# Fourier output product from sums and differences of paired weight rows, in native float32 with the weights stationary

## The reference, cut to what matters

```python
def fourier_mix(h):                      # h: 256 tokens x 2048
    hg = h.reshape(B, L, FNET_GROUPS, FNET_GROUP_DIM)        # 8 groups of 256
    return jnp.fft.fftn(hg, axes=(1, 3)).real.reshape(B, L, D)
...
y_lat = fourier_mix(h_lat) @ fnet_w_out[slot]                # 2048 x 2048 weights
x = x + g1 * rms_norm(y_lat, norm_g[i, 1])
...
h = modulate(rms_norm(x, norm_g[i, 2]), sh2, sc2)            # then the MLP
```

## Time and profile before

| | |
|---|---|
| Time, median of 3 runs | 1682.26 us (1682.08 to 1682.56) |
| Profiled execution, first to last instruction (span) | 1678.7 us |
| PE busy | 1667.0 us, 99% of the span |
| DVE, ACT busy | 1190.8 us, 858.7 us |
| Mean granted clock of TensorE | 0.998 |

### The profile page before, as it was taken

The page is one execution under the profiler, slowest core; times in us unless marked ns, Lnnn a source line. Parts: engine busy times, 40 slices in busy tenths (PEclk is TensorE's granted clock), DMA queues, the critical chain, the costliest instruction groups (busy, mean ns, idle before and its releaser), DMA issues.

```text
span 1678.7 us, 22570 instructions
## 1 busy us (share of the span) xinstructions
PE 1667.0 (99%) x9084; PEld 1444.9 (86%) x9084; DVE 1190.8 (71%) x1291; ACT 858.7 (51%) x1212; POOL 21.3 (1%) x34
## 2 busy tenths in 40 slices
PE   9999999999999999999999999999999999999997
PEld 9899888888989988888898888888888888888886
DVE  7878777887868777798678577777655455546555
ACT  7667556444656655644464564434443444334442
POOL 0000000000100000000000000000000000000000
PEclk9999999999999999999999999999999999999999
DMA  9689676997777777799639478887655665566553
GB/s 333 215 274 313 218 272 226 335 356 279 247 258 253 267 238 263 240 346 370 228 125 334 151 226 282 294 286 245 196 176 200 187 190 197 210 196 188 189 200 126
DMA packets 218120, 408.16 MB, mean 243 GB/s; under 512 B 9088, under 2 KB 87200, under 8 KB 217248
## 3 DMA queue, kind: packets, MB, share of 16 engines
q1 hardware_dynamic: 217520, 404.58, 70.3%
q10 hardware_dynamic: 496, 2.14, 0.3%
HBM read 404.58 MB, written 2.11 MB: 242 GB/s over the span
## 4 chain that ended last, share of the span: by engine, by line
PE 97%; issue 1%; DVE 1%; ACT 0%; DMA 0%; POOL 0%; DVEq 0%; POOLq 0%; SPq 0%; ACTq 0%
PE banks L455 96%; PE banks L1663 1%; PE banks L1625 0%; DMA modw<-in_w_mod 0%; PE banks L1634 0%; DVE X L1104 0%; DVE X L1532 0%; PE banks L1821 0%; POOL sc L674 0%; ACT junk L712 0%; DVE modacc L1139 0%; ACT junk L723 0%; ACT swap L809 0%; ACT vtmp L1017 0%; ACT vtmp L1007 0%
## 5 line engine op out<-in xcount | busy, mean ns | idle before, releaser
L451 DVE TENSOR_TENSOR wlo<-raw,whi 128x1024 fp32r<-128x1024 f32 (+2 forms) x561 | 663.4, 1189 | 375.0 <-ACT whi L444 372.1
L444 ACT ACTIVATE whi<-raw 128x1024 fp32r<-128x1024 f32 (+2 forms) x561 | 573.4, 1030 | 578.4 <-PE banks L455 542.6
L455 PE MATMUL banks<-H,whi 128*128 128x512 f32 x2048 | 660.0, 398 | 0.7 <-DVE H L1062 0.7
L455 PEld LDWEIGHTS banks<-H,wlo 128*128 128x128 f32 x2048 | 384.9, 188 | 88.5
L455 PE MATMUL banks<-whi,Y 128*128 128x512 f32 x1472 | 455.6, 389 | 0.0
L455 PE MATMUL banks<-H,wlo 128*128 128x256 f32 x2048 | 402.6, 278 | 0.0
L455 PEld LDWEIGHTS banks<-whi,Y 128*128 128x128 f32 x1472 | 276.3, 188 | 57.7 <-DVE wlo L451 0.2
L455 PEld LDWEIGHTS banks<-H,whi 128*128 128x128 f32 x2048 | 317.0, 189 | 1.9 <-issue 0.8
L455 PE MATMUL banks<-wlo,Y 128*128 128x512 f32 x768 | 298.8, 389 | 0.0
L1139 DVE SCALAR_TENSOR_TENSOR modacc<-modw,cvx,modacc 128x1024 f32<-128x1024 f32 x188 | 240.4, 1279 | 9.7 <-DMA modw<-in_w_mod 9.4
L455 PEld LDWEIGHTS banks<-wlo,Y 128*128 128x128 f32 x768 | 144.2, 188 | 29.8
(11 more groups left out here) (224 smaller groups left out, 1343.5 us busy)
## 6 DMA issues: line engine op xcount, KB each, us to landing
modw<-in_w_mod SPq DMA_DIRECT2D x192, 512.0 KB, 6.5
raw<-in_w_in SPq DMA_DIRECT2D x72, 1024.0 KB, 5.4
raw<-in_w_mlp_in SPq DMA_DIRECT2D x64, 1024.0 KB, 5.5
raw<-in_w_mlp_out SPq DMA_DIRECT2D x64, 1024.0 KB, 5.0
raw<-in_w_o SPq DMA_DIRECT2D x32, 1024.0 KB, 7.1
raw<-in_w_fnet SPq DMA_DIRECT2D x16, 1024.0 KB, 5.1
raw<-in_w_mv SPq DMA_DIRECT2D x7, 1024.0 KB, 6.3
raw<-in_w_mk SPq DMA_DIRECT2D x6, 1024.0 KB, 6.1
```

Of the source, the lines that this page charges most:

```text
L444: nc.scalar.activation(hi_part(step, n), raw[u % RAW][:, (step % 2) * n:(step % 2) * n + n], ACT.Copy).then_inc(hi_ready, 1)
L451: nc.vector.tensor_tensor(wlo[u % RAW][:, part], raw[u % RAW][:, part], hi_part(step, n).bitcast(F32), ALU.subtract).then_inc(lo_ready, 1)
L455: return nc.tensor.matmul(o, a, b, start=start, stop=stop, skip_group_check=True)
```

## The change

The transform over features now gives, for each of 8 groups, only the outputs 1 to 128 (`PQ`, 32 native matmuls), and 16 more matmuls give output 0 of all groups (`P0`, 8 rows). Since output j and output 256 - j of a group are the same in their cosine part and opposite in their sine part, the product with `w_fnet` takes row j plus row 256 - j against the even part, and row j minus row 256 - j against the odd one. DVE makes these sums and differences (`fold`), and `dscale` halves row 128, which pairs with itself. The matmuls are native float32, with the folded weights stationary, and their result has features on the partitions; so ACT copies it out (`columns_out`), DVE makes all 256 frequencies (`unfold`), and PE transposes it to tokens (`tokens_of`). Rows 255 to 128 of each group are needed against rows 1 to 128, so 32 DMAs of 8 x 4 rows of 8 KB (`turn_rows`) write them in reversed order to `backward` in device memory, one with each of the load units 16 to 47 of layer 1. The product's last quarter is no longer done by token half, and the tail is written in another order. Twelve modulation units stand ahead of the product (`DFT_MODS`) and five in it, instead of 19 in it, and the pass's `mod_sums` stand behind it.

```diff
-BY_TOKEN = (FN_H - 8, ML_H - 8, END_H - 8)
+BY_TOKEN = (FN_H - 8, END_H - 8)
...
+DFT_MODS = [FN_H - 1 + (i + 1) / 16 for i in range(12)]
+TURN_AT = tuple(range(16, 48))
+BEFORE_MLP = ML_H - 0.5
...
-    for s in range(1, 22):
-        if s % 8:
-            yield FN_H + s
+    yield from DFT_MODS
+    for s in (2, 5, 13, 15, 21):
+        yield FN_H + s
...
-IDLE = 24
+IDLE = (12, 2)
...
+        PQ = at("PQ", [P, HEADS, SEQ], 0)
+        P0 = at("P0", [HEADS, SEQ], 16)
+        w0 = at("w0", [HEADS, D], 17)
+        own0 = at("own0", [P, 2 * HEADS], 30)
+        dscale = at("dscale", [P, 2], 30.25)
+        folded = [at(f"folded{i}", [P, 2, UNITW // 4], 96 + 4 * i) for i in range(HIR)]
...
+            if FN_H <= 2 * (u - RAW) < ML_H:
+                sp.wait_ge(fold_ready, 2 * (u - RAW) - FN_H + 2)
...
+            def turn_rows(i):
+                n = P // len(TURN_AT)
+                sp.dma_start(backward[:, i * n:(i + 1) * n, :], w_fnet.rearrange("(h r) n -> h r n", h=HEADS)[
+                    :, SEQ - 1 - i * n:SEQ - 1 - (i + 1) * n:-1, :]).then_inc(vec_in, 16)
...
+                        if l == DEPTH - 1 and at_unit in TURN_AT:
+                            turn_rows(TURN_AT.index(at_unit))
...
+            def load_pairs(v):
+                u, n, i = FN_H // 2 + v, v // 4, v % 4
+                if v < RAW:
+                    sp.wait_ge(half_used, 2 * (u - RAW) + 2)
+                else:
+                    sp.wait_ge(fold_ready, 2 * (v - RAW) + 2)
+                pairs = raw[u % RAW].rearrange("p (h e n) -> p h e n", h=2, e=2)
+                two, cols = slice(2 * i, 2 * i + 2), slice(512 * n, 512 * n + 512)
+                sp.dma_start(pairs[:, :, 0, :], rows_of_head[1:P + 1, two, cols]).then_inc(raw_in[u % RAW], 16)
+                sp.dma_start(pairs[:, :, 1, :], backward.rearrange("h p n -> p h n")[:, two, cols]).then_inc(raw_in[u % RAW], 16)
+            for at_step in DFT_MODS[:3]:
+                load_mod(at_step)
+            sp.wait_ge(vec_in, 32 + 16 * len(TURN_AT))
+            for v in range(16):
+                load_pairs(v)
+                if v == 0:
+                    sp.dma_start(w0[:, :], w_fnet.rearrange("(h r) n -> h r n", h=HEADS)[:, 0, :]).then_inc(vec_in, 16)
+                if v == RAW - 1:
+                    for at_step in DFT_MODS[3:]:
+                        load_mod(at_step)
+                load_mods(FN_H + 2 * v - MOD_LEAD)
...
-            for s in range(AHEAD):
-                split_hi(act, FN_H + s)
...
+            for h in range(HEADS):
+                act.wait_ge(f_ps, h + 1)
+                nc.scalar.activation(PQ[:, h, :], bank(h)[:, 0:SEQ], ACT.Copy, scale=dscale[:, 0:1]).then_inc(f_pq, 1)
+            act.wait_ge(f_ps, HEADS + 1)
+            nc.scalar.activation(P0[:, 0:P + 1], bank(0)[0:HEADS, 0:P + 1], ACT.Copy).then_inc(f_pq, 1)
+            def columns_out(r):
+                act.wait_ge(f_ps, HEADS + 1 + r + 1)
+                if r >= 2:
+                    act.wait_ge(f_mix, r - 1)
+                nc.scalar.activation(flat(pq[:, r % 2, :, :]), bank(4 + r % 4), ACT.Copy).then_inc(f_pq, 1)
+            for n in range(3):
+                columns_out(2 * n)
+                columns_out(2 * n + 1)
+                act.wait_ge(tok_T, n + 1)
+                row_squares([acc[n % 2][:, t * 512:(t + 1) * 512] for t in range(MT)], n)
+                act.wait_ge(row_sq, 2 * (4 * DEPTH + n) + 2)
+                act.sem_inc(acc_act, 1)
+            split_hi(act, ML_H)
+            split_hi(act, ML_H + 1)
+            columns_out(6)
+            columns_out(7)
+            act.wait_ge(tok_T, 4)
             for t in range(MT):
-                token_end(1, t)
                 row_square(acc[1][:, t * 512:(t + 1) * 512], 3, t)
-                x_squares(1, t)
-                if t == 0:
-                    split_hi(act, ML_H)
-                    split_hi(act, ML_H + 1)
             act.wait_ge(row_sq, 2 * 4 * (DEPTH + 1))
             act.sem_inc(acc_act, 1)
+            for t in range(MT):
+                x_squares(1, t)
...
+            for at_step in DFT_MODS[:3]:
+                mod_unit(at_step)
...
+            nc.vector.memset(own0[:, 0:HEADS - 1], 0.0)
+            nc.vector.memset(own0[:, HEADS - 1:HEADS], 1.0)
+            nc.vector.memset(own0[:, HEADS:2 * HEADS], 0.0)
+            nc.vector.tensor_scalar(dscale[:, 0:1], ident[:, P - 1:P], -0.5, 1.0, ALU.mult, ALU.add)
+            def fold(s):
+                v = s // 2
+                dve.wait_ge(raw_in[v % RAW], 16 * (FN_H // 2 // RAW) + 32 * (v // RAW + 1))
+                dve.wait_ge(half_used, free_after(FN_H + s))
+                first, second = (raw[v % RAW][:, 1024 * (s % 2) + 512 * e:1024 * (s % 2) + 512 * e + 512] for e in range(2))
+                tt(folded[s % HIR][:, 0, :], first, second, ALU.add)
+                tt(folded[s % HIR][:, 1, :], first, second, ALU.subtract).then_inc(fold_ready, 1)
+            def unfold(r):
+                dve.wait_ge(f_pq, HEADS + 1 + r + 1)
+                if r >= 2:
+                    dve.wait_ge(tok_T, r // 2)
+                both_out, both = mix[:, r % 2, :, :], pq[:, r % 2, :, :]
+                even, odd = both[:, :, 1:P], both[:, :, P + 1:]
+                nc.vector.tensor_copy(both_out[:, :, 0:P + 1:P], both[:, :, 0:P + 1:P])
+                tt(both_out[:, :, 1:P], even, odd, ALU.subtract)
+                tt(both_out[:, :, SEQ - 1:P:-1], even, odd, ALU.add).then_inc(f_mix, 1)
+            for at_step in DFT_MODS[3:8]:
+                mod_unit(at_step)
...
+            for s in range(AHEAD):
+                fold(s)
+                mod_unit(DFT_MODS[8 + s])
+            mod_unit(DFT_MODS[11])
             for s in range(32):
-                mod_added(FN_H + s)
-                if FN_H + s + AHEAD < ML_H:
-                    split_lo(dve, FN_H + s + AHEAD)
+                if s + AHEAD < 32:
+                    fold(s + AHEAD)
                 mod_step(FN_H + s)
                 if s and s % 8 == 0:
+                    unfold(s // 4 - 2)
+                    unfold(s // 4 - 1)
...
+            split_lo(dve, ML_H)
+            split_lo(dve, ML_H + 1)
+            unfold(6)
+            unfold(7)
+            dve.wait_ge(acc_dve, DVE0 + 3)
+            dve.wait_ge(tok_T, 4)
+            for t in range(MT):
+                dve.wait_ge(row_sq, 2 * (4 * (DEPTH + 1) - 1) + t + 1)
+                nc.vector.tensor_reduce(sc[:, OM + t:OM + t + 1], sc[:, PS + PN * t:PS + PN * t + PN], AX_X, ALU.add).then_inc(o_ms, 1)
+                tt(otok[:, t, 1536:], acc[1][:, t * 512:(t + 1) * 512], rowb[:, 1536:], ALU.mult).then_inc(row_out, 1)
+            def token_mean(t):
+                dve.wait_ge(x_part, 4 + 2 * t + 2)
+                nc.vector.tensor_reduce(sc[:, MS + 2 + t:MS + 3 + t], sc[:, XP + XN * t:XP + XN * t + XN], AX_X, ALU.add).then_inc(x_ms, 1)
+            def normed(t, c):
+                nc.vector.tensor_scalar(xn[:, t, c], X[:, t, c], sc[:, RS + 2 + t:RS + 3 + t], None, ALU.mult).then_inc(x2_xn, 1)
+            low, high = slice(0, D // 2), slice(D // 2, D)
+            for t in range(MT):
+                dve.wait_ge(row_out, 2 + t + 1)
+                dve.wait_ge(o_rstd, DEPTH - 1 + 2 + t + 1)
+                for c in (low, high):
+                    nc.vector.scalar_tensor_tensor(X[:, t, c], otok[:, t, c], sc[:, OR + t:OR + t + 1], X[:, t, c],
+                                                   ALU.mult, ALU.add).then_inc(x_new, 1)
+                    if t and c == low:
+                        token_mean(0)
+            mod_added(BEFORE_MLP + 1)
             dve.wait_ge(mod_out, 3)
             nc.vector.scalar_tensor_tensor(A2[:, :], mod(4), 1.0, ng(2), ALU.add, ALU.mult)
-            dve.wait_ge(acc_dve, DVE0 + 3)
-            for t in range(MT):
-                if t:
-                    split_lo(dve, ML_H)
-                token_residual(1, t, acc[1], rowb)
-                if t:
-                    split_lo(dve, ML_H + 1)
-                token_norm(1, t)
-                for c in XN_PART if t else (slice(0, D // 2), slice(D // 2, D)):
-                    nc.vector.tensor_scalar(xn[:, t, c], X[:, t, c], sc[:, RS + 2 + t:RS + 3 + t], None, ALU.mult).then_inc(x2_xn, 1)
-            dve.wait_ge(row_out, 4)
+            dve.wait_ge(x_rstd, DEPTH + 2 + 1)
+            normed(0, low)
+            token_mean(1)
+            normed(0, high)
+            dve.wait_ge(x_rstd, DEPTH + 2 + 2)
+            for c in XN_PART:
+                normed(1, c)
...
+            for h in range(HEADS):
+                pe.wait_ge(ab_val, h + 1)
+                o = bank(h)
+                for i in range(2):
+                    mm(o[:, 0:P + 1], cs[:, i, 1:P + 1], AB[:, 2 * h + i, even], i == 0, False)
+                    w = mm(o[:, P + 1:SEQ], cs[:, i, SEQ + 1:SEQ + P + 1], AB[:, 2 * h + i, odd], False, i == 1)
                 w.then_inc(f_ps, 1)
-            for s in range(24):
-                n = s // 8
```

(74 more changed lines are left out.)

124 lines of the change are left out of this document (47 added, 77 removed).

## The result

The changed kernel takes **1672.01 us** (median of 4 runs, 1670.34 to 1674.73), the kernel before beside it 1682.41 us: ratio 0.9939, 95% interval 0.9927 to 0.9951. It is faster by 10.4 us where 21.4 were forecast, outside the range. The profiled executions show a difference of 7.8 us in span (1678.7 and 1670.9), so 13.6 us less than forecast, and these can be found one by one. The 7.8 is the smaller figure partly by chance: of the kernel before, the 28 further runs whose span is on record have spans of 1679.0 to 1684.8 us (median 1680.7), each 1.8 us under its own time, so the profiled one is the shortest of all, 2.0 us under that median. The changed kernel's profiled execution lies 0.7 us over its median time. The page answers to the earlier trace rows: ACT has 34 us less, PE 15 us less.

The account below looks back on a forecast made before the run. PE, busy for 99% of the span, was taken to bound the kernel. -103.3 + 74.9 + 1.2 + 5.75 = -21.4 us gave 1660.8 us from 1682.26, range 1656 to 1670.

Parts of the forecast that it names:

- PE removed: Feature transform (14.40 us) and product (88.90 us) leave PE's work, together 103.3 us.
- the rate of native float32: 0.226 us a native matmul, 0.113 a record; a rival had 0.30 and 1685 us, its chance next to nothing.
- PE added: PQ 7.2, P0 3.6, product 57.9, w0 3.6 and transposes 2.6 us, 74.9 together; P0 and w0 at full price.
- DVE ahead of the transform: Ahead of PQ, PE waits 1.2 us for AB additions behind five modulation units; bounds 0 and 4.
- one of the prediction's own signs of being wrong: Waits for folded tiles, for modw, or in layer 1 for DMA adding up to more than 3 us.
- The clock: Tail: clock should hold through 1.2 us of idleness; rival: it falls, 1664 us; clock or longer tail, chance 0.13.
- DVE and loads in the product: DVE's 61.8 us fit beside PE's 64.1, loads hidden, no wait; rival: product held, 1664 to 1676 us, chance 0.08.
- The reversing copies: Layer 1: each copy costs 0.75 us of all engines where 1.35 is free; taken at nothing.
- the mild form of its rival: Layer 1: copies take 1.6 to 2.0 us each, +0 to +12 us, 1663 to 1673; chance 0.08.
- the strong one: Layer 1: copies take 3.0 us each, +44, 1705 us; slower by copies or float32's rate, chance 0.05.
- The estimate that goes by the Trainium skill: Layer 1: only 8 engines work, 1.5 us a copy for 1.35 free, 5 us over all, mostly hidden.
- The tail, +5.75: From the product's end to the MLP's first matmul: longer by 5.75 us, becoming 14.4 us.

Follow-up runs that it names:

- e2: In the changed kernel, w0 and P0 are written as weights of 128 rows instead of 8, the others zeros; 1664.95 us, ratio 0.9899 to the kernel before.
- e3: In the changed kernel, each product quarter's four w0 matmuls come together behind the others, still with 8 rows; 2.1 us less than the changed kernel.
- e4: In the changed kernel, DVE does the AB additions ahead of modulation units that wait for modw, with first folds between these; time fell by 3.8 us.
- e8: In the changed kernel, 18 idle matmuls ahead of PQ and two ahead of the last output transposes; PQ 7.24 us, tail 14.6 us, whole time not given.
- e5: In the changed kernel, the 32 copies are spread over both layers, one for every four load units, with their own semaphore; runs 1668.99 to 1672.88 us.
- e11: In the changed kernel, the 32 copies move 64 of 2048 columns and the second half's rows load unreversed; 1670.92 us.
- e1: The changed kernel without the reversing copies, the backward halves loaded from v4 as they stand; 1670.27 us.
- e10: e6_best with 8 instead of 12 idle tail matmuls and the copies moved to layer 1 stretches with the smallest DMA share before; 1662.16 us.
- e12: e6_best with 8 instead of 12 idle tail matmuls, the copies back at layer 1 units 16 to 47 but issued by GpSimd; 1660.53 us.
- e6_best: e2, e4 and e5 together in the changed kernel, the last two modulation units behind the loop's first two folds; 1659.62 us, ratio 0.9861 to before.
- e9: e6_best with 8 instead of 12 idle tail matmuls and without copies, the second half's rows loaded unreversed; 1658.49 us.

## Why the prediction was wrong, by its steps

*PE removed, and the rate of native float32*: right. 0.113 us a record holds in the transform, in P0 and in the product (116 records in 13.22 us). That term, the largest, kept the sign right.

*PE added: "I take the full price for both"*: right for P0, 128 rows by 8 columns, 3.6 us. For w0 this step failed. The modulation sums, from which the price came, have few columns moving but 128 weight rows, and w0 differs in just the thing that costs. Forecast at 3.6 us, it measured 9.5, mis-sized by 5.9, shown by e2 and e3; the rest of the product came 0.5 under its forecast, which leaves the 5.4. The bounds reached below the full price, not above, although no row showed such weights.

*DVE ahead of the transform: "PE waits 1.2 us"*: right in mechanism and place, 4.55 us in size, over its upper bound of 4. What failed is the start of the chain: the step let the first of the five units begin with the end of the second `csx`, and took 3.9 to 6.5 us as landing times. The first unit waited 2.60 us behind `csx`, because its transfer was issued only at 838.5, behind four pairs of loads in SP's order, and took 8.4 us. The waits for the fourth and fifth, whose transfers landed after some 4 us, the step had. Already of the `modw` transfers issued in 832 to 860 us of the kernel before the trace gives

```profile
DMA to landing us min/median/max: 5.9/7.2/9.2
```

so the longer times could have been read there. e4 shows that the wait goes when DVE's order alone is changed. With a wait for `modw` of more than 3 us, one of the prediction's own signs of being wrong came true.

*The clock*: the rival looked at the tail alone. The fall that cost time stood ahead of PQ, a consequence of the mis-sized wait: +1.8 us, shown by e4 and e8. The idle time was 4.55 us there. With 3.43 us it fell in e3 and e5 as well, 2.7 to 2.8 us after the idle time began and for 6.8 us (PQ over 10 us), but with 3.44, 3.33 and 2.58 us in e11, e1 and e2 it did not. In the tail it fell too, against the forecast, after 0.96 us of idle time ahead of the last transposes and 16 sums with 4 columns each; in the kernel before it stood at 1.00 throughout. That costs nothing when the half clock is short, and 1.6 us when it lasts some 7 us, since 12 idle matmuls then end later than `xn`.

*DVE and loads in the product*: right, no wait of PE there. It is thin: e4 needed only one fold too far back for 1.19 us.

*The reversing copies: "taken at nothing"*: failed, about 2 us, within the mild form of its rival and far from the strong one. The step compared the mean DMA share with the free share. e5, e10, e11 and e12 show that neither mean share nor bytes nor SP's time alone sets the price. The estimate that goes by the Trainium skill ("DMA: Bandwidth & Descriptors", "Why a DMA increments its semaphore by 16 and not by 1"), 5 us with most of it hidden, has the right order, but it is an estimate by bytes, and e11 moved a thirty-second of them for much the same start.

*The tail, +5.75*: right in size, 14.6 for 14.4, and partly by luck. The clock was to hold and did not; it cost nothing because the half clock lasted 3.4 us. Of the eight kernels with 12 idle matmuls and nothing that fills the gap, five had it for 6.8 us and a tail of 16.1 to 16.4.

With wait, clock and w0 repaired e6_best reaches a span of 1658.5 us, 1.2 over the forecast of 1657.3, which had no copies' price in it, and a median of 1659.62, 1.2 under the forecast of 1660.8. The two differ because the forecast set the median 3.6 us over the span, as in the kernel before, whose profiled execution was a short one; the runs of e6_best lie 1.8 over theirs. Either way the rest of the sum stood to about 1 us.

## What to carry to other kernels

Price an operation by a row that has the same number of weight rows, not only the same count of records, and where none does, keep a bound above the full price. Weights of few rows between full ones were cheaper here when padded with zeros (5.9 us for 16), or grouped (4.5). When waits for a DMA stand ahead of work that PE needs, take the landing time from that very stretch, and add what the clock does after the wait. Filling matmuls at a fixed number can become the path when the clock is at half.

## What the runs showed of the hardware

- Going from weights of 128 rows to 8 and back costs 0.37 us with one 8-row matmul between (changed kernel against e2) and 0.34 with four (e3).
- After 3.3 to 3.4 us of idle time the clock fell in two kernels (e3, e5) and not in two others (e1, e11), and at half it lasted some 3.4 us or some 6.8. What decides was not found.
- 32 copies of 256 KB from device memory to device memory raised PE's waits in the stretch around them from 0.3 to 0.7 us (e1, e9) to 1.8 to 2.4; with a thirty-second of the bytes (e11) it was 1.7, from another queue (e12) 2.4. Neither bytes nor queue explains that by itself.
